# One level of Strassen's scheme for the first input projection of a two-layer decoder trunk

## The chip, the core and the metric

The kernel runs on one core of a Trainium2 chip. The time is device microseconds (us) for one execution of the whole program. TensorE (PE) multiplies, VectorE (DVE) and ScalarE (ACT) work elementwise and read the PSUM banks, GpSimd (POOL) works elementwise on SBUF, and SyncE (SP) issues transfers.

## The reference

The trunk has two layers over 512 tokens of width 1024, in float32. Layer 0 begins with the projection that the change rewrites: 1024 inputs to 7168 outputs, split into seven parts.

```python
def conv_gmlp_mixer(xn, w_in, conv_w, ln_g, ln_b, w_s, b_s, w_out):
    proj = xn @ w_in                       # 512 x 1024 times 1024 x 7168
    a_b, a_c, a_x, a_gate, b_u, b_v, b_gate = jnp.split(proj, EVEN_SPLITS, axis=-1)
    y_a = a_b * causal_short_conv(a_c * a_x, conv_w) * jax.nn.silu(a_gate)
    v = layernorm(b_v, ln_g, ln_b).reshape(bsz, n_chunks, B_CHUNK, B_GROUPS, B_GDIM)
    ...
    s = jnp.einsum('gts,bnsgc->bntgc', w_causal, v) + b_s[None, None, :, :, None]
    y_b = b_u * s.reshape(bsz, seq, B_WIDTH) * jax.nn.silu(b_gate)
    return jnp.concatenate([y_a, y_b], axis=-1) @ w_out
```

After it come an output projection, a gated per-layer embedding, and layer 1 (an mLSTM with its own projections), none of whose arithmetic changes.

## The kernel before

Every large product is done in three passes to keep float32 accuracy: a weight `w` is split into `w_hi` (its rounded form, `hi` on ACT, line 453) and `w_lo = w - w_hi` (`lo` on DVE, line 741), the activations likewise into `x_hi` and `x_lo`, and PE adds `hi*hi`, `hi*lo` and `lo*hi` in a PSUM bank.

Weights come in **slots** of 1 MB (128 partitions x 2048 numbers), 87 in all, two in flight (`raw`, `w_hi`, `w_lo` have two places). A slot is 48 matmuls of 128x128 weights against 512 columns. The first 28 slots are the projection: 4 token-major for `b_v` (the result has tokens on partitions, lines 1186 to 1188), then four groups of 4 feature-major slots (`a_c`, `a_x`, `a_gate`, `a_b`, lines 1172 to 1174, 256 features each), then four pairs (`b_gate`, `b_u`), between which PE does 8 small matmuls of the causal mix (line 1263). In feature-major form the convolution along the tokens needs no transpose. `tail(0)`, the output projection, follows.

Each engine's queue is written out by hand, and semaphores join them. `hi(s+2)` and `lo(s+2)` stand in the queues where the slot `s` is being finished, and wait for its last matmul. POOL does only tiny norm arithmetic (lines 384 to 386), the triangle mask of the mix weights (line 404), and so on. SP loads slot `s` when `lo(s-2)` is done.

At the start, the four token tiles of `x` are normalised (`h_square` on ACT, three POOL operations, `normalise` on DVE, line 764), transposed on PE (line 1201, 8 transposes a tile) and split (`x_high` line 473, `x_low` line 771); products of a tile start as soon as it is there.

## Time and profile before

| what | us |
|---|---|
| median of 3 runs | 1057.43 |
| lowest and highest of them | 1055.49 and 1058.51 |
| span of the profiled execution | 1055.9 |
| PE busy in it | 1033.2 (98%) |
| DVE busy | 505.8 (48%) |
| ACT busy | 325.0 (31%) |
| POOL busy | 57.3 (5%) |

The span is one execution under the profiler and lies inside the spread of the runs. A busy PE is not PE at its peak, since matmuls are pipelined and a row's duration (some 0.39 us) is longer than the distance from one matmul's start to the next; the starts are what counts.

### The profile page before, as it was taken

The page shows a single profiled execution, that of the slowest core. Times are in us where ns is not written, and L with a number is a line of the kernel's source. Part 1 is how long each engine was busy: PE and PEld are TensorE (multiplying, and loading weights), DVE is VectorE, ACT ScalarE, POOL GpSimd, SP SyncE. Part 2 cuts the span into 40 slices and gives each one's busy share as a digit, 9 for nine tenths or more (in the row PEclk, how much of TensorE's full clock was granted, in tenths as well). Part 3 has the DMA queues.
Part 4 walks back from the last instruction along what each step waited for, and adds up shares of the span by engine and source line. Part 5 has one row for each costly group of instructions (what it writes and reads, how often), then busy time and mean ns, then how long its engine had stood idle before and what let it go on. Part 6 is the DMA issues. An engine that isn't in the chain of part 4 may idle for free.

```text
span 1055.9 us, 12689 instructions
## 1 busy us (share of the span) xinstructions
PE 1033.2 (98%) x4702; PEld 854.6 (81%) x4702; DVE 505.8 (48%) x748; ACT 325.0 (31%) x556; POOL 57.3 (5%) x107
## 2 busy tenths in 40 slices
PE   6999999999999999998999999999999999999998
PEld 4888888888888888787888888888888888888876
DVE  5244454447664224656554453543355235441735
ACT  5221212122112124544332322332233222322622
POOL 2010000000000002203000000000000000000400
PEclk9999999999999999999999999999999999999999
DMA  7322232322322422221322222123222222143122
GB/s 299 120 92 108 80 120 79 116 82 80 104 95 70 180 109 80 80 95 65 120 80 81 80 80 108 55 81 112 82 79 79 79 80 80 40 180 120 41 80 79
DMA packets 17107, 102.22 MB, mean 97 GB/s; under 512 B 2096, under 2 KB 3120, under 8 KB 5936
## 3 DMA queue, kind: packets, MB, share of 16 engines
q1 hardware_dynamic: 17072, 101.74, 26.5%
q8 instruction: 24, 0.39, 0.2%
q14 instruction: 11, 0.09, 0.0%
HBM read 99.64 MB, written 2.10 MB: 96 GB/s over the span
## 4 chain that ended last, share of the span: by engine, by line
PE 93%; DVE 2%; POOL 2%; ACT 2%; issue 1%; DMA 1%; POOLq 0%; SPq 0%; DVEq 0%; ACTq 0%
PE bank L1174 17%; PE bank L1172 17%; PE bank L1173 17%; PE bank L1186 12%; PE bank L1188 12%; PE bank L1187 12%; PE bank L1415 1%; ACT square L464 1%; PE bank L1406 1%; PE bank L1418 1%; PE bank L1393 1%; POOL rstds L386 1%; PE bank L1263 1%; PE bank L1354 1%; POOL rstds L385 1%
## 5 line engine op out<-in xcount | busy, mean ns | idle before, releaser
L741 DVE TENSOR_TENSOR w_lo<-raw,w_hi 128x1024 fp32r<-128x1024 f32 x174 | 206.3, 1227 | 468.1 <-ACT w_hi L453 468.0
L453 ACT ACTIVATE w_hi<-raw 128x1024 fp32r<-128x1024 f32 x174 | 174.8, 1053 | 568.5 <-PE bank L1174 327.1
L1172 PE MATMUL bank<-x_hi,w_hi 128*128 128x512 f32 x776 | 305.2, 393 | 0.0
L1174 PE MATMUL bank<-x_hi,w_lo 128*128 128x512 f32 x776 | 302.3, 390 | 0.0
L1173 PE MATMUL bank<-x_lo,w_hi 128*128 128x512 f32 x776 | 302.2, 389 | 0.0
L1174 PEld LDWEIGHTS bank<-x_hi,w_lo 128*128 128x128 f32 x776 | 145.6, 188 | 30.5
L1173 PEld LDWEIGHTS bank<-x_lo,w_hi 128*128 128x128 f32 x776 | 145.7, 188 | 30.1
L1172 PEld LDWEIGHTS bank<-x_hi,w_hi 128*128 128x128 f32 x776 | 145.7, 188 | 29.7
L1186 PE MATMUL bank<-w_hi,x_hi 128*128 128x512 f32 x320 | 128.1, 400 | 0.6 <-DVE w_lo L741 0.5
L1187 PE MATMUL bank<-w_lo,x_hi 128*128 128x512 f32 x320 | 125.9, 393 | 0.0
L1188 PE MATMUL bank<-w_hi,x_lo 128*128 128x512 f32 x320 | 125.8, 393 | 0.0
L1186 PE MATMUL bank<-w_hi,y_hi 128*128 128x512 f32 x256 | 100.1, 391 | 0.0
L1188 PE MATMUL bank<-w_hi,y_lo 128*128 128x512 f32 x256 | 99.6, 389 | 0.0
L1187 PE MATMUL bank<-w_lo,y_hi 128*128 128x512 f32 x256 | 99.6, 389 | 0.0
L1186 PEld LDWEIGHTS bank<-w_hi,x_hi 128*128 128x128 f32 x320 | 61.0, 191 | 13.7 <-issue 0.8
L1188 PEld LDWEIGHTS bank<-w_hi,x_lo 128*128 128x128 f32 x320 | 60.9, 190 | 13.0
L1187 PEld LDWEIGHTS bank<-w_lo,x_hi 128*128 128x128 f32 x320 | 61.1, 191 | 12.4
L1188 PEld LDWEIGHTS bank<-w_hi,y_lo 128*128 128x128 f32 x256 | 48.0, 188 | 10.0
L1187 PEld LDWEIGHTS bank<-w_lo,y_hi 128*128 128x128 f32 x256 | 48.1, 188 | 9.9
L1186 PEld LDWEIGHTS bank<-w_hi,y_hi 128*128 128x128 f32 x256 | 48.1, 188 | 9.8
L384 POOL TENSOR_TENSOR rstds<-sums 128x1 f32<-128x1 f32 x24 | 12.0, 499 | 487.6 <-ACT square L464 487.6
L1201 PE MATMUL bank<-ident,scaled 128*128 128x128 f32 x128 | 19.0, 296 | 16.4 <-DVE scaled L764 12.7
(145 smaller groups left out, 755.5 us busy)
## 6 DMA issues: line engine op xcount, KB each, us to landing
...
```

The source lines that it names most:

```text
L384: link(pool.tensor_tensor(dst, first, second, ALU.add))
L385: link(pool.tensor_scalar(dst, dst, 1.0 / D, EPS, ALU.mult, ALU.add))
L386: pool.tensor_tensor(dst, dst, minus_half[:, 0:1], ALU.pow).then_inc(done, 1)
L453: act.activation(w_hi[:, r, c], raw[:, r, c], ACT.Copy).then_inc(hi_ready, 1)
L741: dve.tensor_tensor(w_lo[:, r, c], raw[:, r, c], w_hi[:, r, c].bitcast(F32), ALU.subtract).then_inc(lo_ready, 1)
L1172: pe.matmul(bank[b][:, :], w[0][:, k, at], x_hi[:, k], start=(k == 0), stop=False)
L1173: pe.matmul(bank[b][:, :], w[0][:, k, at], x_lo[:, k], start=False, stop=False)
L1174: done = pe.matmul(bank[b][:, :], w[1][:, k, at], x_hi[:, k], start=False, stop=(k == KD - 1))
L1186: pe.matmul(bank[b][:, :], hi_[:, k0 + k, tt], w[0][:, k, c], start=(start and k == 0), stop=False)
L1187: pe.matmul(bank[b][:, :], hi_[:, k0 + k, tt], w[1][:, k, c], start=False, stop=False)
L1188: done = pe.matmul(bank[b][:, :], lo_[:, k0 + k, tt], w[0][:, k, c], start=False, stop=(stop and k == ks - 1))
L1201: done = pe.transpose(bank[norm_bank(e, t) + q][:, k * P:(k + 1) * P], scaled[:, t % 2, (4 * q + k) * P:(4 * q + k + 1) * P], ident[:, :])
```

## The change

The projection becomes seven **units** of 1024 output columns. One unit is a 512 x 1024 times 1024 x 1024 product cut in half in each dimension, and computed with seven block products instead of eight. The weight quarters are called X, V, Z, Y (buffers `BX`, `BV`, `BZ`, `BY`). Products 1, 2 and 3 use X, Z and Y as loaded. The other four need block sums, made in place in `raw7`:

- product 5: X + V, by a POOL add of 128x2048 numbers
- product 6: that sum + Y, by a second POOL add
- product 7: V + Y, by a transfer from POOL's queue that adds Y onto V (`accum_op`)
- product 4: sum 6 + Z, by a second such transfer (`late_sum`)

A product is 24 matmuls of 512 columns (2 token tiles, 4 blocks of the inner dimension, 3 passes). It is token-major in all seven units, so x is the stationary side. The order in a unit is 1, 5, 6, 2, 3, 7, 4 (in the first 1, 2, 5, 6, 3, 7, 4). Weight splits (`hi7`, `lo7`) run two products ahead in a ring of three. The sums of results are kept in PSUM and in `s5`: `b_copy` and `s5_copy` on ACT, `c_make` and `s5_make` on DVE. `s5_make` reads product 7's result, and product 4 waits for it, which is next in PE's queue.

The seven left-side blocks (`l_hi`, `l_lo`) are made once at the start; four of them are sums and differences of x blocks made on DVE. Since `a_c * a_x` and the gates are now token-major, PE transposes them (`conv_transposes`, 8 for each of 8 feature tiles), and the mixed half as well (`mix_transposes`, 4 for each of 8). The causal mix is 8 matmuls of 512 columns instead of 32 of 128. The layer norm's scale and shift, on DVE before, are now 16 POOL operations of 128x512 (`ln_affine`). Two matmuls (`warm`) stand between the first two tiles' transposes. `h` is loaded again for the residual, because its place is used. The hi and lo of the mixer's outputs are made in the last unit and in `tail(0)`.

The weights of the projection are read as 4 MB for a unit as before, and the two adding transfers read 2 MB more. Nothing in layer 1 or in the output projection changes but where tensors lie.

The core of the diff:

```diff
+UNITS = 7
+ORDER_FIRST = (1, 2, 5, 6, 3, 7, 4)
+ORDER = (1, 5, 6, 2, 3, 7, 4)
+L_PLACE = {1: 0, 5: 1, 6: 2, 2: 3, 3: 4, 7: 5, 4: 6}
+RING = 3
+ROWS_IN = 4 * UNITS
+KIND = "vaaaabb"
...
+def source(u, p):
+    return {1: x_buffer(u), 5: s5_buffer(u), 6: x_buffer(u), 2: BZ, 3: BY, 7: BV, 4: x_buffer(u)}[p]
...
+        def block_in(u, b):
+            row_of = {BX: 0, BV: 1, BZ: 2, BY: 3}
+            sp.dma_start(raw7[:, x_buffer(u) if b == BX else b], slots[4 * u + row_of[b]]).then_inc(b_in[b], 16)
...
+        for u in range(UNITS):
+            sp.wait_ge(sum_done, sum_at(u, 6))
+            sp.wait_ge(w7_lo_ready, split_done(u, 5))
+            if u + 1 < UNITS:
+                block_in(u + 1, BX)
+            sp.wait_ge(w7_lo_ready, split_done(u, 2))
+            if u + 1 < UNITS:
+                block_in(u + 1, BZ)
+            sp.wait_ge(w7_lo_ready, split_done(u, 3))
+            if u + 1 < UNITS:
+                block_in(u + 1, BY)
+            else:
+                load(0, 0, wait=False)
+                load(1, 1, wait=False)
+            sp.wait_ge(w7_lo_ready, split_done(u, 7))
+            if u + 1 < UNITS:
+                block_in(u + 1, BV)
...
+        def add(u, p, dst, one, two):
+            if p == 5:
+                pool.wait_ge(b_in[BX], 16 * (u + 1))
+                pool.wait_ge(b_in[BV], 16 * (u + 1))
+                if u:
+                    pool.wait_ge(w7_lo_ready, split_done(u - 1, 4))
+            if p == 6:
+                pool.wait_ge(sum_done, sum_at(u, 5))
+                pool.wait_ge(b_in[BY], 16 * (u + 1))
+                pool.wait_ge(w7_lo_ready, split_done(u, 1))
+            pool.tensor_tensor(raw7[:, dst], raw7[:, one], raw7[:, two], ALU.add).then_inc(sum_done, 1)
+        def sums_of(u):
+            add(u, 5, s5_buffer(u), x_buffer(u), BV)
+            add(u, 6, x_buffer(u), s5_buffer(u), BY)
+            pool.wait_ge(sum_done, sum_at(u, 5))
+            pool.dma_start(raw7[:, BV], slots[4 * u + 3], accum_op=ALU.add).then_inc(added_in[7], 16)
+        def late_sum(u):
+            pool.wait_ge(w7_lo_ready, split_done(u, 6))
+            pool.dma_start(raw7[:, x_buffer(u)], slots[4 * u + 2], accum_op=ALU.add).then_inc(added_in[4], 16)
...
+                pool.wait_ge(ln_in, 32)
+                pool.wait_ge(vst_ready, TILES)
+            link(pool.tensor_tensor(v_even[:, g], v_even[:, g], over_tiles(ln_g), ALU.mult))
+            pool.tensor_tensor(v_even[:, g], v_even[:, g], over_tiles(ln_b), ALU.add).then_inc(ln_done, 1)
...
+            if p in SUMS:
+                act.wait_ge(sum_done, sum_at(u, p))
+            elif p in added_in:
+                act.wait_ge(added_in[p], 16 * (u + 1))
+            else:
+                act.wait_ge(b_in[BX if p == 1 else source(u, p)], 16 * (u + 1))
+            if g >= RING:
+                act.wait_ge(prod_done, 2 * (g - RING) + 2)
+            for half in range(2):
+                c = slice(half * SLOT // 2, (half + 1) * SLOT // 2)
+                act.activation(w7_hi[:, g % RING, c], raw7[:, source(u, p), c], ACT.Copy).then_inc(w7_hi_ready, 1)
...
+        def b_copy(u, tp):
+            act.wait_ge(prod_done, 2 * STEP[u, 1] + tp + 1)
+            if u:
+                act.wait_ge(b_free, 2 * (u - 1) + tp + 1)
+            else:
+                act.wait_ge(warm, 1)
+            act.activation(b_of(tp)[:, :], a_of(tp)[:, :], ACT.Copy).then_inc(b_copied, 1)
+        def s5_copy(u, tp):
+            act.wait_ge(prod_done, 2 * STEP[u, 5] + tp + 1)
+            if u:
+                act.wait_ge(s5_made if u == 1 else s5_free, s5_used(max(u - 1, 1), tp))
+            act.activation(s5[:, tp], c_of(tp)[:, :], ACT.Copy).then_inc(s5_copied, 1)
...
+        def lo7(g):
+            if g >= RING:
+                dve.wait_ge(prod_done, 2 * (g - RING) + 2)
+            for half in range(2):
+                c = slice(half * SLOT // 2, (half + 1) * SLOT // 2)
+                dve.wait_ge(w7_hi_ready, 2 * g + half + 1)
+                dve.tensor_tensor(w7_lo[:, g % RING, c], raw7[:, source(*STEPS[g]), c],
+                                  w7_hi[:, g % RING, c].bitcast(F32), ALU.subtract).then_inc(w7_lo_ready, 1)
...
+        def c_make(u, tp):
+            dve.wait_ge(s5_copied, 2 * u + tp + 1)
+            dve.wait_ge(prod_done, 2 * STEP[u, 6] + tp + 1)
+            dve.tensor_tensor(c_of(tp)[:, :], s5[:, tp], b_of(tp)[:, :], ALU.subtract).then_inc(c_made, 1)
+        def s5_make(u, tp):
+            dve.wait_ge(prod_done, 2 * STEP[u, 7] + tp + 1)
+            dve.wait_ge(c_made, 2 * u + tp + 1)
+            if KIND[u] == "v":
+                dve.tensor_tensor(v_even[:, 4:8, 2 + tp, :], s5[:, tp].rearrange("p (g c) -> p g c", g=4),
+                                  four(b_of(tp)), ALU.subtract).then_inc(s5_made, 1)
+            else:
+                dve.tensor_tensor(s5[:, tp], s5[:, tp], b_of(tp)[:, :], ALU.subtract).then_inc(s5_made, 1)
...
+            if k == 0:
+                left_sum(5, f5)
+                dve.wait_ge(full_ready[11], 2)
+                dve.wait_ge(full_ready[5], 2)
+                dve.tensor_tensor(f21[:, :, :], f11[:, :, :], f21[:, :, :], ALU.subtract).then_inc(full_ready[7], 1)
+                dve.wait_ge(full_ready[7], 1)
+                dve.tensor_tensor(f11[:, :, :], f5[:, :, :], f11[:, :, :], ALU.subtract).then_inc(full_ready[6], 1)
+                dve.wait_ge(full_ready[6], 1)
+                dve.wait_ge(full_ready[12], 2)
+                dve.tensor_tensor(f12[:, :, :], f11[:, :, :], f12[:, :, :], ALU.add).then_inc(full_ready[3], 1)
+                left_sum(6, f11)
...
+                if k == 3:
+                    for tp in range(2):
+                        c_make(u, tp)
+                if k == 6:
+                    s5_make(u, 1)
+                if g + 2 < 7 * UNITS:
+                    lo7(g + 2)
+                else:
+                    lo(k - 5)
...
+                if k == 4:
+                    for tp in range(2):
+                        if now == "a":
+                            z_make(u, a_of, tp, tp, a_free)
+                        else:
+                            wide_silu(u, a_of, tp, tp, a_free)
+                if was == "a" and k in (2, 4):
+                    conv(2 * (u - 2) + (k - 2) // 2)
...
+                if k == 5:
+                    s5_make(u, 0)
+                if k == 6:
+                    for tp in range(2):
+                        if now == "a":
+                            g_make(u, c_of(tp), tp, tp, c_free)
+                        else:
+                            gu_make(u, c_of(tp)[:, :], tp, tp, a_free, c_free)
...
+            first = p in (1, 5)
+            tt = slice(tp * P, (tp + 1) * P)
+            for k in range(4):
+                if tp == 0 and k % 2 == 0:
+                    pe.wait_ge(w7_lo_ready, 2 * g + k // 2 + 1)
+                c = slice(k * SEQ, (k + 1) * SEQ)
+                left_hi, left_lo = l_hi[:, L_PLACE[p], k, tt], l_lo[:, L_PLACE[p], k, tt]
+                pe.matmul(dst[:, :], left_hi, w7_hi[:, r, c], start=(first and k == 0), stop=False,
+                          skip_group_check=True)
+                pe.matmul(dst[:, :], left_hi, w7_lo[:, r, c], start=False, stop=False, skip_group_check=True)
+                done = pe.matmul(dst[:, :], left_lo, w7_hi[:, r, c], start=False, stop=(k == 3),
+                                 skip_group_check=True)
+            done.then_inc(prod_done, 1)
...
+            for t in range(TILES):
+                done = pe.transpose(bank[6][:, t * P:(t + 1) * P], z_tok[:, t, f * P:(f + 1) * P], ident[:, :])
+            done.then_inc(zt_ready, 1)
+            pe.wait_ge(c_free, 2 * v + 2)
+            pe.wait_ge(s5_free, s5_used(v, 1))
+            if n:
+                pe.wait_ge(y32_a, n)
+            for t in range(TILES):
+                done = pe.transpose(bank[7][:, t * P:(t + 1) * P], g_tok[:, t, f * P:(f + 1) * P], ident[:, :])
+            done.then_inc(gt_ready, 1)
...
+        first_transpose(0)
+        for tp in range(2):
+            done = pe.matmul(b_of(tp)[:, :], ident[:, :], h[:, 0, 0:SEQ], start=True, stop=True)
+        done.then_inc(warm, 1)
+        first_transpose(1)
+        product(0, 1, 0)
+        first_transpose(2)
+        product(0, 1, 1)
+        first_transpose(3)
+        for g in range(1, 7 * UNITS):
+            u, p = STEPS[g]
+            k = g % 7
+            if u and KIND[u - 1] == "a" and k in (2, 4):
+                conv_transposes(2 * (u - 2) + (k - 2) // 2)
+            if u == UNITS - 1:
+                if k >= 3:
+                    mix_transposes(k - 3)
+                if 2 <= k <= 5:
+                    mix(k - 2)
+            for tp in range(2):
+                product(u, p, tp)
...
+    def quarters(c1, c2):
+        for half in (slice(0, SEQ), slice(SEQ, D)):
+            for c in (c1, c2):
+                token(c, half, slice(0, SEQ))
```

**DVE, unit 3 of the projection (its feature group before).** Before, two slots of `lo`, and the convolution of two tiles:

```order
L741 TENSOR_TENSOR w_lo<-raw,w_hi 128x1024 [waits hi_ready,product_ready]
L741 TENSOR_TENSOR w_lo<-raw,w_hi 128x1024 [waits hi_ready]
L827 TENSOR_TENSOR conv_in<-bank,act_t 128x512 [waits act_freed,product_ready] x2
L836 TENSOR_SCALAR acc<-conv_in,conv_sb 128x512 [waits dve_freed]
L838 SCALAR_TENSOR_TENSOR acc<-conv_in,conv_sb,acc 128x512 [waits dve_step] x2
```

Now, from product 3 to product 4 of a unit (`s_85` is `s5`, `y_78` is `y32`; lines of the changed kernel):

```order
L1088 TENSOR_TENSOR w_lo<-raw_75,w_hi 128x1024 [waits w7_hi_ready,prod_done]
L1088 TENSOR_TENSOR w_lo<-raw_75,w_hi 128x1024 [waits w7_hi_ready]
L1165 TENSOR_TENSOR z_tok<-bank,ac_s 128x256 [waits zt_ready,ac_ready] x2
L1182 TENSOR_SCALAR y_78<-conv_in,conv_sb 128x512 [waits conv_ready]
L1184 SCALAR_TENSOR_TENSOR y_78<-conv_in,conv_sb,y_78 128x512 [waits dve_step] x2
L1186 TENSOR_TENSOR y_78<-y_78,bank 128x512 [waits gt_ready,dve_step]
L1088 TENSOR_TENSOR w_lo<-raw_75,w_hi 128x1024 [waits w7_hi_ready,prod_done]
L1088 TENSOR_TENSOR w_lo<-raw_75,w_hi 128x1024 [waits w7_hi_ready]
L1154 TENSOR_TENSOR s_85<-s_85,bank 128x512 [waits c_made,prod_done] x2
```

The step that PE waits for (line 1154) stands behind two splits and a convolution.

**POOL, after the first unit.** Before, behind the first tiles' norms stood one mask and more norm steps:

```order
L404 AFFINE_SELECT wt<-wt 128x1024 [waits const_in]
L408 TENSOR_SCALAR rstds<-bn_mv 128x1 [waits ln_stats]
L409 TENSOR_TENSOR rstds<-rstds,minus_half 128x1 [waits pool_step]
```

Now each unit has two wide adds and two transfers, and units 2, 3 and 4 have layer norm pairs too (`raw_75` is `raw7`):

```order
L521 TENSOR_TENSOR raw_75<-raw_75 128x2048 [waits w7_lo_ready,v_raw_in,x_raw_in]
L521 TENSOR_TENSOR raw_75<-raw_75 128x2048 [waits w7_lo_ready,y_raw_in,sum_done]
L527 DMA raw_75<-in_slots 128x2048 [waits sum_done]
L531 DMA raw_75<-in_slots 128x2048 [waits w7_lo_ready]
L558 TENSOR_TENSOR v_even<-v_even,ln_g 128x512 [waits vst_ready,ln_in]
L559 TENSOR_TENSOR v_even<-v_even,ln_b 128x512 [waits pool_step]
```

POOL's first add of unit u+1 waits for the weight split of product 4 of unit u, the first two rows of the DVE piece above.

**DVE at the start.** Before, between the fourth tile's scaling and the second slot's split:

```order
L764 SCALAR_TENSOR_TENSOR scaled<-h,rstds,g_pre 128x1024 [waits xt_ready,pre_rstd]
L771 TENSOR_TENSOR x_lo<-bank,x_hi 128x4x128 [waits xhi_ready] x2
L741 TENSOR_TENSOR w_lo<-raw,w_hi 128x1024 [waits hi_ready] x2
```

Now, up to the split of the third product's weights:

```order
L1095 SCALAR_TENSOR_TENSOR scaled<-h,rstds,g_first 128x1024 [waits first_xt,first_rstd]
L1108 TENSOR_TENSOR l_lo<-bank,l_hi 128x4x128 [waits lhs_hi4]
L1117 TENSOR_TENSOR f_83<-f_81,bank 128x4x128 [waits first_xt,full21_ready]
L1088 TENSOR_TENSOR w_lo<-raw_75,w_hi 128x1024 [waits w7_hi_ready] x2
L1108 TENSOR_TENSOR l_lo<-bank,l_hi 128x4x128 [waits lhs_hi4]
L1117 TENSOR_TENSOR f_83<-f_81,bank 128x4x128 [waits first_xt,full21_ready]
L1121 TENSOR_TENSOR l_lo<-f_83,l_hi 128x1024 [waits lhs_hi5]
L1220 TENSOR_TENSOR f_81<-f_80,f_81 128x1024 [waits full5_ready,full11_ready]
L1222 TENSOR_TENSOR f_80<-f_83,f_80 128x1024 [waits full7_ready]
L1225 TENSOR_TENSOR f_82<-f_80,f_82 128x1024 [waits full12_ready,full6_ready]
L1121 TENSOR_TENSOR l_lo<-f_80,l_hi 128x1024 [waits lhs_hi6]
L1121 TENSOR_TENSOR l_lo<-f_82,l_hi 128x1024 [waits lhs_hi3]
```

All of these come before the weights of the third product are split on DVE.

## Rows read from the trace of the kernel before

**Rows 1.** The page's parts 1 and 4: busy times, and the chain by engine.

```profile
PE 1033.2 (98%) x4702; PEld 854.6 (81%) x4702; DVE 505.8 (48%) x748; ACT 325.0 (31%) x556; POOL 57.3 (5%) x107
...
PE 93%; DVE 2%; POOL 2%; ACT 2%; issue 1%; DMA 1%; POOLq 0%; SPq 0%; DVEq 0%; ACTq 0%
```

**Rows 2.** Busy time by stretch: stretch, length, PE, PEld, DVE, ACT, POOL, clock, DMA.

```profile
142.00:183.00 41.00, 41.00 (x182) 33.95 (x182) 18.04 (x24) 8.08 (x10) 0.00 (x0) 1.00 0.29 102
```

**Rows 3.** Timeline, PE at the projection's end: start, duration, engine, line, operation.

```profile
330.61 0.39 PE L1186 MATMUL bank<-w_hi,y_hi 128*128 128x512 f32 x1
```

**Rows 4.** Timeline, ACT: weight splits, one for each finished slot.

```profile
192.80 2.01 ACT L453 ACTIVATE w_hi<-raw 128x1024 fp32r<-128x1024 f32 x2 [7.90 <-PE bank L1174]
203.68 2.01 ACT L453 ACTIVATE w_hi<-raw 128x1024 fp32r<-128x1024 f32 x2 [8.87 <-PE bank L1174]
...
294.57 2.00 ACT L453 ACTIVATE w_hi<-raw 128x1024 fp32r<-128x1024 f32 x2 [8.87 <-PE bank L1174]
...
318.13 2.00 ACT L453 ACTIVATE w_hi<-raw 128x1024 fp32r<-128x1024 f32 x2 [8.87 <-PE bank L1174]
```

**Rows 5.** Timeline, PE at the start.

```profile
17.95 0.63 PE L1188 MATMUL bank<-w_hi,x_lo 128*128 128x512 f32 x1
18.38 0.62 PE L1186 MATMUL bank<-w_hi,x_hi 128*128 128x512 f32 x1
...
19.07 0.39 PE L1188 MATMUL bank<-w_hi,x_lo 128*128 128x512 f32 x1
19.30 1.03 PE L1201 MATMUL bank<-ident,scaled 128*128 128x128 f32 x8
20.09 0.47 PE L1186 MATMUL bank<-w_hi,x_hi 128*128 128x512 f32 x1
20.40 0.39 PE L1187 MATMUL bank<-w_lo,x_hi 128*128 128x512 f32 x1
```

**Rows 6.** Groups by line and form: count, then busy us, mean ns, idle before.

```profile
L741 DVE TENSOR_TENSOR w_lo<-raw,w_hi 128x1024 fp32r<-128x1024 f32 x174 | 206.3, 1227 | 468.1 <-ACT w_hi L453 468.0
L453 ACT ACTIVATE w_hi<-raw 128x1024 fp32r<-128x1024 f32 x174 | 174.8, 1053 | 568.5 <-PE bank L1174 327.1 <-PE bank L1188 225.6 <-DMA raw<-in_slots 15.8
...
L771 DVE TENSOR_TENSOR x_lo<-bank,x_hi 128x512 fp32r<-128x512 f32 x32 | 20.4, 683 | 0.6 <-ACT x_hi L473 0.5
...
L464 ACT ACTIVATE square<-h 128x512 f32<-128x512 f32 x32 | 20.2, 630 | 10.4 <-DVE h L930 5.4 <-DMA h<-in_x 4.4
...
L473 ACT ACTIVATE x_hi<-bank 128x512 fp32r<-128x512 f32 x32 | 17.8, 613 | 9.0 <-PE bank L1201 9.0
...
L838 DVE SCALAR_TENSOR_TENSOR acc<-conv_in,conv_sb,acc 128x512 f32<-128x512 f32 x16 | 12.0, 752 | 1.9 <-DVE acc L836 0.5 <-DVE acc L838 0.2
...
L836 DVE TENSOR_SCALAR acc<-conv_in,conv_sb 128x512 f32<-128x512 f32 x8 | 3.9, 482 | 0.8 <-DVE acc L838 0.7
```

**Rows 7.** Timeline, DVE at the start.

```profile
16.39 1.28 DVE L764 SCALAR_TENSOR_TENSOR scaled<-h,rstds,g_pre 128x1024 f32<-128x1024 f32 x1 [1.00 <-POOL rstds L386]
17.59 1.28 DVE L771 TENSOR_TENSOR x_lo<-bank,x_hi 128x512 fp32r<-128x512 f32 x2
18.79 1.28 DVE L764 SCALAR_TENSOR_TENSOR scaled<-h,rstds,g_pre 128x1024 f32<-128x1024 f32 x1
...
22.00 3.28 DVE L741 TENSOR_TENSOR w_lo<-raw,w_hi 128x1024 fp32r<-128x1024 f32 x2
...
30.85 2.36 DVE L741 TENSOR_TENSOR w_lo<-raw,w_hi 128x1024 fp32r<-128x1024 f32 x2 [4.06 <-ACT w_hi L453]
```

**Rows 8.** Timeline, POOL at the start.

```profile
16.69 1.04 POOL L384 TENSOR_TENSOR rstds<-sums 128x1 f32<-128x1 f32 x1 [0.34 <-ACT square L464]
...
18.09 0.55 POOL L386 TENSOR_TENSOR rstds<-rstds,minus_half 128x1 f32<-128x1 f32 x1
...
21.97 1.10 POOL L404 TENSOR_SCALAR_AFFINE_SELECT wt<-wt 128x1024 f32<-128x1024 f32 x1 [3.34 <-DMA bias_sb<-in_gate_bias]
```

**Rows 9.** Transfers of the tile `raw`, window 95 to 330 us.

```profile
DMA to landing us min/median/max: 4.7/4.8/6.6
```

929 lines of the change are left out of this document (601 added, 328 removed).

## The prediction

> **What bounds the kernel now.** I read the busy times and the chain by engine first [rows 1]: PE is busy 98% of the span and the chain is PE for 93% of it. In the projection, PE is never idle in a 41 us stretch while DVE works 18.0 us and ACT 8.1 [rows 2]. So work taken from PE is worth its full time, as long as what PE waits for arrives. Next the pitch: one slot is finished every 203.68 - 192.80 = 10.88 us, that is 48 matmuls of 0.2267 us [rows 4]. The projection ends at 330.61, where the output projection's first matmul starts [rows 3]. Of that, 28 slots are 28 x 10.88 = 304.6. Two of the last slots with their 8 mix matmuls between take 318.13 - 294.57 = 23.56, so the mix costs 1.8 us, 7.2 in four groups [rows 4]. The remaining 330.6 - 304.6 - 7.2 = 18.8 us is the start: loads, norms, transposes, and matmuls that start 0.43 us apart (17.95 to 18.38) until 18.4 and 0.23 apart from about 19 [rows 5], the lower and the higher level of PE's clock.
>
> **PE's own work after the change.** 49 products of 24 matmuls are 49 x 5.44 = 266.6 us, 38.1 less. New are 96 transposes. Eight of them lie between the matmul start at 19.07 and the one at 20.09; less one matmul of 0.23, and with the next start 0.08 late, that is 0.87 us or 0.11 each [rows 5]: 10.5 us. The mix has the same number of columns, 7.2 us. Together 284.3 against 311.8, so **27.5 us less**, if nothing waits. The 16 transposes and 4 mix matmuls that now lie inside the output projection are in this sum. I cost the `y` splits there at nothing: four slots of products (43.5 us) lie over them, and ACT and DVE need under 15; without that cover it would be PE's wait for the last of them, some 3 us.
>
> **The start.** The third product (5) needs block sums of x, and in DVE's queue these stand before the split of its weights (last piece of the order). The third tile's scaling starts at 16.39 in the trace [rows 7]. Two more ACT copies (0.61 each [rows 6]) stand ahead of its squares; since POOL's steps there waited for DVE anyway, I add 0.4 of their 1.2. Behind its squares ACT now makes four copies before the fourth tile's two squares (0.63 each, 1.6 with their reads) [rows 6], so the fourth scaling starts at 16.8 + 2.4 + 1.6 = 20.8 (18.79 before [rows 7]). Then come in turn: the scaling 1.28, four PSUM-reading steps 2.73, a split 2.36, ACT's pass of 1.05, four DVE passes of 1.23 (4.9), ACT's next pass and half split 2.1, DVE's half split 1.2, gaps 0.5; 16.1 in all [rows 6, 7], while the two remaining `l_lo` passes run beside ACT. Product 5 starts at 37.0. Two products, 10.9 us, lie before it, so the start costs 26.1 instead of 18.8, **7.3 us more**. The two `warm` matmuls fall in the wait for the second tile; each is four times a mix matmul, 0.9 us, or 1.8 at the low clock, so their cost is up to 3.6 us, and their gain up to 2, if the first product then runs at the high one. I take zero.
>
> **The adds on POOL.** No row shows an add of 128x2048 on POOL. The nearest is the mask of 128x1024, with one input: 1.10 us [rows 8]. By it a 2048-wide operation is 2.1 us if both inputs come at once, and 4.2 if one after the other. I take 4.2, since the inputs are two; the lower bound is 2.1. GPSIMD Engine Reference, Instruction dispatch, in the Trainium skill says that both inputs share one read port and gives some 2.5 cycles per element; at its 1.2 GHz that is an estimate of 4.3 us for an add, and the sum below would be 0.7 higher by it. No run here shows it.
>
> What the adds do to DVE is in the trace. While the mask ran on POOL (21.97 to 23.07), two halves of `lo` took 3.28 us instead of 2.36 [rows 7, 8]: 0.92 lost of 1.10. The reverse too: POOL's tiny add at 16.69 took 1.04 us and ended with DVE's scaling (16.39 to 17.67), while the next, at 18.09, took its usual 0.55 beside DVE's `x_low` (17.59 to 18.87), which has a PSUM input [rows 7, 8]. So a DVE operation with two SBUF inputs, and a POOL operation, exclude each other; one with a PSUM input is free. By this, at the start, both adds (8.4 us), which start when the fourth tile's norm is done, fall into the DVE chain above; two PSUM-reading steps of 0.68 hide 1.4. **7.0 us more.**
>
> **Inside a unit.** With product 1 at 0, products end every 5.44, plus 0.9 for 8 transposes before the third and the fifth: product 3 ends at 29.0, product 7 at 34.4, where product 4 wants `s5_make`. DVE's queue there (the second piece of the order): the split for product 4 begins when ACT's `hi7` is half done behind its copies and the convolution's, at about 25.2, and ends at 27.6; two `z_make` of 0.43 (256 wide, from the 1024- and 512-wide rows) to 28.5; the convolution 0.48 + 2 x 0.75 + 0.68 and gaps, 3.1, to 31.6; the split 2.36 to 34.0; `s5_make` 0.68 to 34.7 [rows 6]. So without POOL PE waits some 0.2, over seven units 1.2.
>
> The next unit's first add waits for the split that ends at 27.6 and for V, whose load goes out after the split for product 7 (22.5) and lands 4.8 us later, at 27.3 [rows 9]. It holds DVE out from 27.7 to 31.9. `z_make` reads PSUM and goes on; the convolution starts at 31.9 instead of 28.5, **3.4 us late**, and so does `s5_make`, with no slack before it. Product 4 and what is behind it on PE wait 3.3. The second add falls after the last split and delays only work with over 5 us of slack. Five units (1 to 5) have a next unit and a convolution or a norm of like size there: 5 x 3.3 = **16.5**. In units 2 and 3, six POOL operations of the layer norm (1.1 each by the mask's row, for two inputs of a quarter of the add's width) alternate with DVE before `c_make`; I take 1.5 each, **3.0**, between 0 and 6.
>
> **Sum.** -27.5 + 7.3 + 7.0 + 16.5 + 3.0 + 1.2 = +7.5. The profiled span is 1055.9, so 1063.4; the median of the runs lies 1.5 above that span, so **1065**. Its own range is 1056 to 1075: the norm term, the 0.92 of 1.10, and the warm matmuls. That one 1.1 us operation keeps DVE out says little of a 4.2 us one: SBUF — State Buffer, Who interferes with whom, in the Trainium skill says that the port is held for the whole instruction. By that the forecast's sum holds; by a port that is handed over in between it would be the second rival's.
>
> **Rivals.**
> - *Short adds.* If an add takes 2.1, the start loses 2.8 instead of 7.0 and a unit 1.3 instead of 3.3; the norms 1. Then -27.5 + 7.3 + 2.8 + 6.5 + 1 + 1.2 = -8.7: 1049. For: half the width costs 1.1. Against: two inputs. V landing late (maximum 6.6 [rows 9]) does not help, since the add then meets the split; it must land 6 us late to miss `s5_make`.
> - *No exclusion in the place that counts,* since POOL's long operation lets DVE in, or DVE's slack is larger than I find. Only the start's chain stays: -27.5 + 7.3 + 1.2 = -19: 1038. Against it stand the 0.92 us.
> - *The adding transfers are late.* Their speed is in no row. A plain 1 MB lands in 4.8 us [rows 9]. The one for product 4 goes out after the split for product 6 (about 7) and `hi7` wants it at 23.9: 17 us of room, and it shares the engines with four plain loads a unit. From 17 us, 3.5 times a plain one, PE waits. At 20 us it is 3 us in each of six units, 18 on top of the forecast: 1083.
>
> **Chances.** Forecast 0.44, short adds 0.22, no exclusion 0.14, late transfers 0.20. A difference of 0.3% (3.2 us) is about what a measurement of this kernel can tell from no change. Faster by more (under 1054.3) holds all of the second rival and most of the first: 0.33. Within: 0.13, the rest of the first and the forecast's lower edge. Slower: 0.54. The range 1040 to 1084 leaves out about half of the second rival and some of the third.
>
> **What would show it.** The start: product 5's first matmul near 44 us if the adds hit, 37 if not. In a unit: POOL's row of the add near 4.2 us; DVE's `TENSOR_SCALAR` of the convolution starting when the add ends; PE idle 3 us before product 4, released by `s5_make`. PE waits of another kind, for `hi7` behind a transfer on POOL's queue, are the third rival. It would be wrong if the add is short, if PE's clock falls to its low level in the long waits at the start (24 matmuls there would cost 5 us more), or if the waits on PE come from ACT's copies, which I hid.

## The result, and the profile after

The changed kernel takes 1076.14 us (median of four runs, 1074.89 to 1076.47) against 1057.29 for the kernel before (median of four runs, one more than above): ratio 1.0183, 95% interval 1.0167 to 1.0198. It is 18.9 us slower, where 7.6 slower was forecast, and lies inside the wide range (1040 to 1084) but just above the forecast's own, 1056 to 1075. The profiled span is 1073.8 us, 17.9 above that of before, and the working below is made in spans.

The page's parts 1 and 4 of the changed kernel, beside [rows 1]:

```profile
PE 1021.1 (95%) x4586; PEld 836.7 (78%) x4586; DVE 618.4 (58%) x809; ACT 406.1 (38%) x680; POOL 162.3 (15%) x151
...
PE 84%; DVE 7%; issue 3%; ACT 3%; POOL 2%; DMA 0%; POOLq 0%; DVEq 0%; ACTq 0%
```

PE is busy 12 us less, yet the span is 18 longer: PE waits, and the chain now runs through DVE for 7% of the span. Two stretches say where, the one of [rows 2] and nearly the whole projection (stretch, length, PE, PEld, DVE, ACT, POOL, clock, DMA):

```profile
142.00:183.00 41.00, 37.77 (x168) 30.93 (x167) 34.22 (x34) 17.55 (x26) 20.33 (x10) 0.96 0.51 138
```

```profile
50.00:304.00 254.00, 233.49 (x1000) 190.56 (x999) 207.67 (x204) 106.65 (x146) 97.75 (x47) 0.94 0.51 140
```

PE has lost 3.2 of 41 us to waiting, DVE's busy time has gone from 18.0 to 34.2, and the granted clock is no longer 1.00. The waits of PE from 46 to 346 us (for what: us in total, times, longest):

```profile
PE bank L1697 <- DVE s L1154: 15.9, 5, 3.4
PE bank L1697 <- issue: 4.6, 2, 3.8
```

L1697 is a product's first kind of matmul, L1154 is `s5_make`: these are the five waits before product 4 that the prediction forecast. One of them in full, with what follows, on PE's timeline:

```profile
113.55 0.79 PE L1697 MATMUL bank<-w_hi,l_hi 128*128 128x512 f32 x1 [3.39 <-DVE s L1154]
114.14 0.63 PE L1699 MATMUL bank<-w_lo,l_hi 128*128 128x512 f32 x1
...
118.83 0.53 PE L1697 MATMUL bank<-w_hi,l_hi 128*128 128x512 f32 x1
119.20 0.40 PE L1699 MATMUL bank<-w_lo,l_hi 128*128 128x512 f32 x1
119.44 0.40 PE L1700 MATMUL bank<-w_hi,l_lo 128*128 128x512 f32 x1
```

From 114.14 to 118.83 the matmuls start 0.43 us apart, which is the level of 1.2 GHz; from 119.20 on 0.23 to 0.24 apart, that of 2.4 GHz. The 12 matmuls from 113.55 on take 118.83 - 113.55 = 5.3 us instead of 12 x 0.2267 = 2.7. So behind a wait of 3.39 us PE loses another 2.6 us. The prediction had no term for this.

What held `s5_make` in the next unit, on DVE's and on POOL's timeline:

```profile
148.98 0.75 DVE L1165 TENSOR_TENSOR z_tok<-bank,ac_s 128x256 f32<-128x256 f32 x2
149.65 0.48 DVE L1182 TENSOR_SCALAR y<-conv_in,conv_sb 128x512 f32<-128x512 f32 x1
150.16 5.78 DVE L1184 SCALAR_TENSOR_TENSOR y<-conv_in,conv_sb,y 128x512 f32<-128x512 f32 x2
155.97 0.69 DVE L1186 TENSOR_TENSOR y<-y,bank 128x512 f32<-128x512 f32 x1
156.58 2.35 DVE L1088 TENSOR_TENSOR w_lo<-raw,w_hi 128x1024 fp32r<-128x1024 f32 x2
158.85 1.28 DVE L1154 TENSOR_TENSOR s<-s,bank 128x512 f32<-128x512 f32 x2
160.05 5.84 DVE L1088 TENSOR_TENSOR w_lo<-raw,w_hi 128x1024 fp32r<-128x1024 f32 x2
```

```profile
149.96 4.64 POOL L521 TENSOR_TENSOR raw<-raw 128x2048 f32<-128x2048 f32 x1 [12.21 <-DMA raw<-in_slots]
159.10 4.57 POOL L521 TENSOR_TENSOR raw<-raw 128x2048 f32<-128x2048 f32 x1 [4.50 <-DVE w_lo L1088]
```

Two convolution steps that take 0.75 each alone [rows 6] take 5.78: the first of them waits for the end of the add at 154.60. The split at 160.05 waits in the same way for the second add. `s5_make`, which reads PSUM, starts at 158.85 and runs undisturbed past 159.10, the start of that add.

At the end of unit 0 the same, first POOL's row and then DVE's:

```profile
61.74 4.58 POOL L521 TENSOR_TENSOR raw<-raw 128x2048 f32<-128x2048 f32 x1 [12.67 <-DMA raw<-in_slots]
```

```profile
62.27 6.27 DVE L1088 TENSOR_TENSOR w_lo<-raw,w_hi 128x1024 fp32r<-128x1024 f32 x2
68.46 1.27 DVE L1151 TENSOR_TENSOR v_even<-s,bank 128x512 f32<-128x512 f32 x2
```

L1151 is unit 0's `s5_make`. PE waits 3.84 us for it before 69.24, listed under "issue" above.

The start, rows of PE, DVE and POOL that answer to [rows 5], [rows 7] and [rows 8]:

```profile
34.41 0.76 PE L1697 MATMUL bank<-w_hi,l_hi 128*128 128x512 f32 x1 [7.43 <-ACT bank L706]
...
42.37 0.47 PE L1697 MATMUL bank<-w_hi,l_hi 128*128 128x512 f32 x1 [0.93 <-DVE w_lo L1088]
```

```profile
19.37 5.58 DVE L1095 SCALAR_TENSOR_TENSOR scaled<-h,rstds,g_first 128x1024 f32<-128x1024 f32 x1 [0.57 <-POOL rstds L496]
...
26.07 5.47 DVE L1088 TENSOR_TENSOR w_lo<-raw,w_hi 128x1024 fp32r<-128x1024 f32 x2
```

```profile
19.30 10.02 POOL L521 TENSOR_TENSOR raw<-raw 128x2048 f32<-128x2048 f32 x2
```

A scaling of 1.28 us takes 5.58 and a split of 2.36 takes 5.47 while both adds run. Product 5 starts at 42.37. Last, the output projection's first matmul, which stood at 330.61 [rows 3]:

```profile
345.84 0.39 PE L1616 MATMUL bank<-w_hi,y_hi 128*128 128x512 f32 x1
```

So the projection is 15.2 us longer and all behind it, with its 16 transposes and 4 mix matmuls, 728.0 instead of 725.3.

### The profile page after: what moved, and what is told of

The parts are those of the page before. It is cut to its first block, busy times and chain, and to the rows that moved or that the text cites. A ratio compares the mean times of both kernels' runs of the same rounds, so it can differ in the third digit from the quotient of the medians.

```text
span 1073.8 us, 12432 instructions
## 1 busy us (share of the span) xinstructions
PE 1021.1 (95%) x4586; PEld 836.7 (78%) x4586; DVE 618.4 (58%) x809; ACT 406.1 (38%) x680; POOL 162.3 (15%) x151
## 4 chain that ended last, share of the span: by engine, by line
PE 84%; DVE 7%; issue 3%; ACT 3%; POOL 2%; DMA 0%; POOLq 0%; DVEq 0%; ACTq 0%
PE bank L1616 10%; PE bank L1618 10%; PE bank L1617 10%; PE bank L1599 8%; PE bank L1600 8%; PE bank L1601 8%; PE bank L1697 7%; PE bank L1700 7%; PE bank L1699 7%; DVE w_lo L1088 2%; ACT square L632 1%; PE bank L1927 1%; DVE y L1184 1%; PE bank L1918 1%; PE bank L1930 1%
## 5 line engine op out<-in xcount | busy, mean ns | idle before, releaser
L1047 DVE TENSOR_TENSOR w_lo<-raw,w_hi 128x1024 fp32r<-128x1024 f32 x118 | 139.2, 1221 | 314.9 <-ACT w_hi L621 314.9
L1697 PE MATMUL bank<-w_hi,l_hi 128*128 128x512 f32 x392 | 162.3, 414 | 28.9 <-DVE s L1154 15.9
L1088 DVE TENSOR_TENSOR w_lo<-raw,w_hi 128x1024 fp32r<-128x1024 f32 x98 | 152.0, 1592 | 50.5 <-ACT w_hi L659 49.9
L1700 PE MATMUL bank<-w_hi,l_lo 128*128 128x512 f32 x392 | 157.8, 403 | 0.0
L1699 PE MATMUL bank<-w_lo,l_hi 128*128 128x512 f32 x392 | 157.8, 402 | 0.0
L1599 PE MATMUL bank<-x_hi,w_hi 128*128 128x512 f32 x392 | 155.6, 397 | 0.0
L1601 PE MATMUL bank<-x_hi,w_lo 128*128 128x512 f32 x392 | 152.6, 389 | 0.0
L1600 PE MATMUL bank<-x_lo,w_hi 128*128 128x512 f32 x392 | 152.5, 389 | 0.0
L1697 PEld LDWEIGHTS bank<-w_hi,l_hi 128*128 128x128 f32 x392 | 77.2, 197 | 49.3 <-DVE s L1154 18.0
L1699 PEld LDWEIGHTS bank<-w_lo,l_hi 128*128 128x128 f32 x392 | 77.4, 197 | 16.8 <-issue 1.0
L1700 PEld LDWEIGHTS bank<-w_hi,l_lo 128*128 128x128 f32 x392 | 76.6, 195 | 16.8
```

Source lines behind the costliest of these rows:

```text
L1047: dve.tensor_tensor(w_lo[:, r, c], raw[:, r, c], w_hi[:, r, c].bitcast(F32), ALU.subtract).then_inc(lo_ready, 1)
L1088: dve.tensor_tensor(w7_lo[:, g % RING, c], raw7[:, source(*STEPS[g]), c], w7_hi[:, g % RING, c].bitcast(F32), ALU.subtract).then_inc(w7_lo ...
L1599: pe.matmul(bank[b][:, :], w[0][:, k, at], x_hi[:, k], start=(k == 0), stop=False)
L1600: pe.matmul(bank[b][:, :], w[0][:, k, at], x_lo[:, k], start=False, stop=False)
L1601: done = pe.matmul(bank[b][:, :], w[1][:, k, at], x_hi[:, k], start=False, stop=(k == KD - 1))
L1697: pe.matmul(dst[:, :], left_hi, w7_hi[:, r, c], start=(first and k == 0), stop=False, skip_group_check=True)
```

## Experiments

Each edit is made to the changed kernel (1076.14 us) unless another is named. Lines in the diffs are shortened to what counts; line numbers shift by a few from kernel to kernel.

### The adds of unit 0 alone, and those of the other units

```diff
+            w = 8 if u == 0 else SLOT      # the other kernel: u > 0
+            pool.tensor_tensor(raw7[:, dst, 0:w], raw7[:, one, 0:w], raw7[:, two, 0:w], ALU.add)
```

> In unit 0 both POOL adds are cut from 2048 to 8 columns (the weights of products 5 and 6 there are not the sums, so the output differs); all else as in the changed kernel (1076.1 us). Theory (in the start chain every POOL add keeps DVE out for its 4.6 to 5.4 us, and PE's clock falls to its low level in the waits that follow): product 5, whose first matmul was at 42.4 us, starts near 36, and the time is 6 to 8 us less, about 1069. Rival A (the start is bound by ACT's and DVE's own copies, the adds hidden beside them): product 5 still near 42, time within 1 us of 1076. Rival B (only the waits before product 4 matter): the same, 1076.

Measured: 1069.13 us, 7.0 less; product 5 starts at 35.14. The chain of the start, forecast at 37.0 without the adds and 44 with them, is shown in its parts: the adds cost 7.2 there.

> The twelve POOL adds of units 1 to 6 are cut to 8 columns (weights of products 5 and 6 there are not the sums); unit 0's stay. Theory: the five waits before product 4 (15.9 us together), the one at the end of unit 0 (3.8 at 69.2 us) and one of 0.7 at 54 go, less about 1.2 that DVE's queue costs by itself; with them goes what the low clock costs behind each (13 matmuls at 0.43 us for 0.23 is 2.7 us, three times that and three times about half of it, 12 in all): 31 us less, about 1045. Rival A (the waits cost only their own length, the low clock is made good elsewhere): 19 less, 1057. Rival B (DVE's queue is late by its own work, not by POOL): at most 4 less, 1072 or more.

Measured: 1044.12 us, 32.0 less, ratio to before 0.9876 (0.9858 to 0.9895). In this trace PE has no wait behind product 5 but two listed under "issue", 0.9 us together, and the granted clock of the same stretch is

```profile
50.00:304.00 254.00, 253.08 (x1146) 208.20 (x1145) 191.29 (x235) 128.16 (x176) 45.68 (x48) 1.00 0.59 160
```

Both rivals fall: DVE's queue is in time by itself, and the waits cost more than their length. Product 5 starts and the projection ends at

```profile
42.35 0.47 PE L1698 MATMUL bank<-w_hi,l_hi 128*128 128x512 f32 x1
...
312.25 0.39 PE L1617 MATMUL bank<-w_hi,y_hi 128*128 128x512 f32 x1
```

These 269.9 us are the 47 products with their transposes and mixes, and the 0.9 us of waits: 269.0 of work. Of those waits 0.77 us come before 54.24, and the changed kernel has the same one (0.74 before 54.27), so that one does not come from the adds of units 1 to 6. In the changed kernel the same stretch takes 345.84 - 42.37 = 303.5. That is 34.5 us over the work; 15.9 + 4.6 = 20.5 are waits, and 14.0 are left for the low clock.

### The waits filled

```diff
+                if 1 <= u < UNITS - 1 and tp == 0:
...
+                    for n in range(12):
+                        pe.matmul(bank[6][:, :], l_hi[:, L_PLACE[4], 0, 0:P], w7_hi[:, r, 0:SEQ], start=True, stop=True,
...
                 pe.wait_ge(s5_made, 2 * u + tp + 1)
```

> Nothing of the work is changed; in units 1 to 5 PE does 12 matmuls into an unused bank (12 x 0.227 = 2.7 us) before it waits for s5_make. Theory (PE's clock falls because PE stands idle in that wait): no low clock after the waits of units 1 to 5, matmuls behind product 4's start 0.23 us apart instead of 0.43, waits themselves shorter only by what the extra matmuls fill; 2.7 + 3 x 1.3 + 2.7 = 9 us less, about 1067. Rival A (the clock falls for another reason, such as the time since the start): the waits are filled but the granted clock still falls, 1076 or up to 3 more. Rival B (the extra matmuls run past the end of the wait): each adds up to 2 us, 1078 to 1086.

Measured: 1068.16 us, 8.0 less. PE at the place of the row of 113.55 above and at the projection's end, and the clock of the stretch:

```profile
109.92 2.88 PE L1693 MATMUL bank<-w_hi,l_hi 128*128 128x512 f32 x12
113.47 0.50 PE L1704 MATMUL bank<-w_hi,l_hi 128*128 128x512 f32 x1 [0.67 <-DVE s L1154]
113.81 0.40 PE L1706 MATMUL bank<-w_lo,l_hi 128*128 128x512 f32 x1
114.04 0.40 PE L1707 MATMUL bank<-w_hi,l_lo 128*128 128x512 f32 x1
...
336.09 0.39 PE L1616 MATMUL bank<-w_hi,y_hi 128*128 128x512 f32 x1
```

```profile
50.00:304.00 254.00, 246.12 (x1103) 201.76 (x1101) 217.39 (x212) 111.48 (x153) 100.79 (x48) 0.99 0.53 144
```

Sixty matmuls more, and the kernel is 8 us faster. Product 4 starts when it started before (113.47 for 113.55), but now at 0.23 us a matmul. The projection ends at 336.09 instead of 345.84, 9.8 us earlier; what lies behind it took 729.4 us in this trace instead of 727.9, with the same work, so the stretch says more here than the whole time.

The low clock can be counted on PE's timeline, as the distance from start to start, less idle time and less 0.2267 us, summed over the matmuls that start late behind a wait. In the changed kernel this gives 11.3 us behind the five waits (2.9, 1.9, 1.7, 1.6 and 3.2) and 2.9 behind that of unit 0. In e3 the five are down to 1.4, which is 9.9 less and as much as the projection gained; unit 0's wait was not filled, and 1.9 remain there. So the six waits account for all of the 14.0 us.

What a wait costs in this way is not fixed by its length. In the trace of e1 a wait of 3.39 us before 105.54, at the same place in unit 1 as the one before 113.55, is followed by matmuls 0.23 us apart and costs 0.3 us more, as in e3. What decides between 0.3 and 3.2 us is not shown by these runs.

### What stands in DVE's queue where the add falls

In the first kernel the first `s5_make` of a unit goes one place forward, ahead of the split for the next unit's product 1, and the convolution one place back, behind that split; the second `s5_make` stays where it was:

```diff
+                if k == 5:
+                    s5_make(u, 0)
                 if k == 6:
                     s5_make(u, 1)
                 if g + 2 < 7 * UNITS:
                     lo7(g + 2)
...
-                if was == "a" and k in (2, 4):
-                    conv(2 * (u - 2) + (k - 2) // 2)
+                if was == "a" and k in (2, 5):
+                    conv(2 * (u - 2) + k // 5)
```

> DVE's queue alone is changed: s5_make stands ahead of the split for the next unit's product 1, and the second convolution of a unit (in unit 1 the norm's last step) behind that split; the adds and everything else stay. Theory (the add's cost is one of place: it pushes what stands between it and s5_make): the six waits before product 4 or its like go, and with them the low clock, and the split for the next product 1 still ends over 2 us before it is wanted; 15.9 + 3.8 + 12 = 31 less, about 1045. Rival A (DVE as a whole has no room, the wait turns up before product 1 or 5 of the next unit as w_lo): half or less of it comes back, 1060 to 1076. Rival B (low clock not tied to these waits): 1057.

Measured: 1083.28 us, 7.1 more. A miss. PE's waits, and DVE and POOL in one unit:

```profile
PE bank L1697 <- DVE s L1154: 26.2, 5, 5.6
```

```profile
151.12 2.35 DVE L1088 TENSOR_TENSOR w_lo<-raw,w_hi 128x1024 fp32r<-128x1024 f32 x2
...
153.90 5.71 DVE L1184 SCALAR_TENSOR_TENSOR y<-conv_in,conv_sb,y 128x512 f32<-128x512 f32 x2
...
160.25 0.68 DVE L1154 TENSOR_TENSOR s<-s,bank 128x512 f32<-128x512 f32 x1
```

```profile
153.64 4.64 POOL L521 TENSOR_TENSOR raw<-raw 128x2048 f32<-128x2048 f32 x1 [2.42 <-DVE w_lo L1088]
```

Only the first `s5_make` had got ahead of the convolution. The second stood behind it, and the second add, released by the split that now stood ahead of the convolution, fell on the convolution. The next kernel moves both and leaves the convolution alone:

```diff
-                if k == 6:
+                if k == 5:
+                    s5_make(u, 0)
                     s5_make(u, 1)
                 if g + 2 < 7 * UNITS:
                     lo7(g + 2)
```

> Only DVE's queue is changed, and less of it than in e5: both s5_make stand ahead of the split for the next unit's product 1, the convolution stays where it was. e5 showed what happened there: its convolution stood ahead of the second s5_make, and the second add (153.64 to 158.28) fell on it. Theory: the first add still pushes the convolution, which then ends near 35.0 in a unit where product 4 wants s5_make at 34.4, so PE waits 0.7 to 1.5 us instead of 3.2, too short for the clock to fall; the second add falls behind both s5_make. 15.9 + 3.8 - 6 x 1.2 + 10 of low clock = 22 less, about 1054. Rival A (the second add now hits the splits of the next unit's products 1 and 5, which have no room): PE waits for w_lo there, 1065 or more. Rival B (the clock falls in waits of 1 us too): 1064.

Measured: 1062.31 us, 13.8 less where 22 were expected. The waits for `s5_make` are down to 3.0 us in two, but others have come: 6.2 us for the mix (`yb`) and 2.3 for the convolution (`y`). They are waits for DVE's late work, as in rival A, but not the ones for `w_lo` that it named, of which there are 0.5 us. Rival B's time is near, 1064, but not its reason: behind the two waits of 1.5 us for `s5_make` the matmuls start 0.23 us apart. In this place too, then, DVE's queue has no room for both adds. The next run tries a third place, behind both `s5_make`:

```diff
                     pool.wait_ge(w7_lo_ready, split_done(u - 1, 4))
+                    pool.wait_ge(s5_made, 2 * u)
```

> One wait more on POOL: the first add of units 1 to 6 waits for both s5_make of the unit before; DVE's queue is as in the changed kernel. Theory (the port is the matter, and where the adds fall sets the cost): no wait before product 4; both adds now lie at 35 to 44 us of a unit, in front of the splits for products 5 and 6 of the next, whose first halves are wanted at 45.3 and 50.7 and come at 45.3 and 50; PE waits 0 to 1.5 us a unit, 31 less plus 6 x 0.8: about 1050. Rival A (no room there either): over 2.5 us a unit and the clock falls again, 1068 or more. Rival B (the adds weren't what held s5_make): 1076.

Measured: 1069.35 us, 6.8 less, by the size that rival A named. Most of the waits have gone to bank c, whose last reader stands behind the split for product 5:

```profile
PE bank L1698 <- DVE g_tok L1173: 8.5, 4, 2.4
...
PE bank L1721 <- DVE y L1187: 4.1, 2, 2.1
```

### Is it the inputs that take POOL's time?

```diff
-            pool.tensor_tensor(raw7[:, dst], raw7[:, one], raw7[:, two], ALU.add)
+            pool.tensor_scalar(raw7[:, dst], raw7[:, one], 1.0, None, ALU.mult)
```

> Each of the 14 POOL adds becomes a multiplication by 1.0 of the same 128x2048, with one input instead of two (the sums are left out, so the output differs). If POOL's time goes by the inputs that it reads, one takes 2.2 to 2.4 us instead of 4.6 (the mask's 128x1024 took 1.10), the waits before product 4 fall from 3.2 to about 1 us, the clock stays high, and the start loses 4.5: about 27 less, 1049. If it goes by the elements written, it takes 4.6 and the time stays at 1076.

Measured: 1077.92 us (two runs). Neither forecast of the operation's length holds: it is longer than the add, with a median of 5.37 us (4.58 for the add):

```profile
L521 POOL TENSOR_SCALAR raw<-raw 128x2048 f32<-128x2048 f32 x14 | 77.1, 5508 | 108.9 <-DVE w_lo L1088 71.0 <-DMA raw<-in_slots 37.7
```

Whether two inputs cost twice as much can't be read from this form, but my reason for 4.2 us, twice the mask's rate because there are two inputs, has lost its ground: another operation with one input takes more. That the figure came out near the add's was luck as far as this reason goes.

### Smaller pieces

```diff
+            for q in range(4):
+                c = slice(q * SEQ, (q + 1) * SEQ)
+                done = pool.tensor_tensor(raw7[:, dst, c], raw7[:, one, c], raw7[:, two, c], ALU.add)
```

> Each add of the changed kernel is four of 128x512 in a row, the first start and the last end as one. If the two engines take turns and neither's work overlaps the other's, DVE's five operations with SBUF inputs between the split and s5_make meet all four pieces one after the other: the same 4.6 us, the same waits, 1076 within 2 us, with DVE's convolution steps each some 1.1 us longer instead of one 4 us longer. If shorter pieces let DVE run beside them, the waits before product 4 fall below 2 us and the clock stays high: 1060 or less.

Measured: 1063.84 us (two runs, 1063.18 and 1064.51), 12.3 less, between the two forecasts. DVE, then POOL (six pieces in one row), in the unit that follows 178 us:

```profile
185.87 2.46 DVE L1187 SCALAR_TENSOR_TENSOR y<-conv_in,conv_sb,y 128x512 f32<-128x512 f32 x2
188.36 0.69 DVE L1189 TENSOR_TENSOR y<-y,bank 128x512 f32<-128x512 f32 x1
188.96 3.83 DVE L1091 TENSOR_TENSOR w_lo<-raw,w_hi 128x1024 fp32r<-128x1024 f32 x2
```

```profile
186.14 11.39 POOL L523 TENSOR_TENSOR raw<-raw 128x512 f32<-128x512 f32 x6 [12.67 <-DMA raw<-in_slots]
```

The convolution pair loses 2.46 - 1.54 = 0.9 us and the split 3.83 - 2.36 = 1.5, 2.4 together where a whole add took 4.2 from the convolution pair alone. This is the mildest unit of the trace for PE: one unit earlier the same steps lose 1.9 and 1.5, 3.3 together. The two engines take turns, and the pieces that fall under DVE's steps with a PSUM input (0.69 us here, and `s5_make`) cost it nothing. With a whole add those steps stand in the queue behind the blocked one and hide nothing. The waits for `s5_make` fall from 15.9 to 11.1 us, and the one at the end of unit 0 from 3.84 to 0.40; the low clock behind them falls too.

### The adds by DVE itself

DVE makes the first sum of the next unit behind the second `s5_make`, the second behind the two steps that free bank c:

```diff
+                if k == 6 and u + 1 < UNITS:
+                    add(u + 1, 5)
+                    for tp in range(2):
+                        g_make(u, c_of(tp), tp, tp, c_free)    # or gu_make
+                    add(u + 1, 6)
                 lo7(g + 2)
```

> The same sums, all made by DVE: the first of the next unit behind the second s5_make, the second behind the two steps that free bank c; POOL keeps its transfers and norms. Theory (POOL's add holds DVE out for 4.6 us, while DVE would need two halves' 2 x 1.2 = 2.4 us for it): 2.2 us less of DVE's time for each add, and none of it ahead of s5_make; no wait before product 4, PE waits under 0.5 us a unit; at the start the chain before product 5 carries one add of 2.4 instead of 10 us: product 5 near 37.5. 32 less for the units and 5 for the start, about 1040. Rival A (DVE has no room, its queue is what binds): waits for w_lo or bank b before products 1, 5 or 6, 1060 or more. Rival B (POOL runs beside DVE at no cost and takes work from it): 1076 + 14 x 2.4 x the share on the path, over 1080.

Measured: 1040.82 us, ratio to before 0.9841 (0.9815 to 0.9866). It beats both kernels, and 1040 was forecast. At the start, where DVE makes unit 0's two adds among its passes, product 5 starts at 35.91 instead of 42.37. Of PE's waits from 46 to 350 us one is left, before product 3 of unit 0 and not before a product 4:

```profile
PE bank L1706 <- issue: 2.8, 1, 2.8
```

And DVE's adds in one unit:

```profile
138.65 1.38 DVE L1154 TENSOR_TENSOR s<-s,bank 128x512 f32<-128x512 f32 x2
139.94 2.28 DVE L1089 TENSOR_TENSOR raw<-raw 128x2048 f32<-128x2048 f32 x1
...
143.72 2.28 DVE L1089 TENSOR_TENSOR raw<-raw 128x2048 f32<-128x2048 f32 x1
```

An add costs DVE 2.28 us when DVE makes it. When POOL makes it, DVE's operations in the rows above take 3.1 to 4.3 us longer. Giving the adds to POOL spared DVE nothing.

### The start

In the first kernel, on top of e8, ACT's two `b_copy` go ahead of the pass for product 5, and the splits for products 5 and 6 come right behind what these need. The second adds to it that `s5_copy` and `c_make` of unit 0 no longer stand behind the split for product 7.

```diff
-                left_sum(5, f5)
                 b_copy(0, 0)
                 b_copy(0, 1)
+                left_sum(5, f5)
+                hi7(2)
                 left_sum(6, f11)
+                hi7(3)
```

> e8 with the start in another order. ACT makes the two bank copies ahead of the pass for product 5's left side, in e8 they stood behind it and PE waited 4.4 us for them (26.96). On DVE and ACT the splits of product 5's and 6's weights come right behind what those products need, the later sums of x behind them. Theory (the start is bound by the queues of DVE and ACT, step by step): product 2 starts near 24.2, after a wait of under 2 us and at the high clock; product 5 near 30 instead of 35.9; product 6 waits for its split until 38, 3.3 less than in e8: 1037.5. Rival A (something else, such as the copies themselves, binds): as e8, 1041. Rival B (product 3 then waits for what was put back, as long as was gained): 1040 to 1044.

Measured: 1041.31 us, as e8. Product 5 starts at 30.14, as forecast (35.91 in e8), but rival B is what happened, in PE's row at product 3:

```profile
50.41 0.77 PE L1712 MATMUL bank<-w_hi,l_hi 128*128 128x512 f32 x1 [6.40 <-DVE bank L1147]
```

In e8 product 3 starts at 50.16. All that was gained before it was lost in one wait for `c_make`.

```diff
                 left_sum(3, f12)          # DVE
+                c_make(0, 0)
+                c_make(0, 1)
```

> e9, and in unit 0 ACT copies product 5's bank right behind the split of product 3's weights, and DVE makes both c_make ahead of the split for product 7's; in e9 the first c_make stood behind it, at 49.62, and PE waited 6.4 us for it from 43.9. Theory (the start's gain of e9 was given back in that one wait): product 3 starts near 45 instead of 50.3, and no wait over 2.5 us follows; 5 less, 1036. Rival A (the next step of the chain, the split of product 7's weights or its left side, is as late): 1039 to 1041. Rival B (what PE gains here it loses before product 4 of unit 0, where V's transfer sets the pace): 1041.

Measured: 1035.00 us, ratio to before 0.9803 (0.9789 to 0.9817), the fastest. Product 3 starts at 45.42, and of PE's waits behind 20 us these are left, and 0.2 under "issue":

```profile
PE bank L1711 <- DVE w_lo L1076: 3.0, 2, 2.5
PE bank L1711 <- ACT bank L691: 1.3, 1, 1.3
```

Last, on the changed kernel itself, the warm matmuls in another place:

```diff
-        done = pe.matmul(b_of(tp)[:, :], ident[:, :], h[:, 0, 0:SEQ], start=True, stop=True)
         first_transpose(1)
         product(0, 1, 0)
         first_transpose(2)
         product(0, 1, 1)
+        done = pe.matmul(b_of(tp)[:, :], ident[:, :], h[:, 0, 0:SEQ], start=True, stop=True)
         first_transpose(3)
```

> The changed kernel with its two warm matmuls moved from ahead of the second tile's transposes to ahead of the fourth's, where PE waits 3.5 us. They must run somewhere, since product 6 adds onto a bank that ACT has filled. Theory (the prediction's zero: what they win by raising the clock early, PE later stands waiting for): the first product's matmuls start 0.43 apart, it ends 2.5 us later, and all of it is lost in the wait for the fourth tile; product 5 at 42.4 as before and 1076 within 1 us. Rival (an early high clock is worth its time): 1078 to 1079.

Measured: 1075.37 us, the same within the spread (1074.65 to 1079.90). The first product's matmuls start 0.43 apart from 15.09 to 17.22 (0.23 in the changed kernel), and PE still waits for the fourth tile (0.83 us before 25.05, where it was 3.50 before 25.00). Product 5 starts at 42.42, where it was 42.37. The zero for the warm matmuls was right. The profiled execution is the longest of the four, but what makes it longer lies behind the start: 731.2 us behind the projection instead of 727.9, with the same work, and 0.6 more in the wait at the end of unit 0.

## Why the prediction was right or wrong

The direction, and the mechanism and place of the waits, were right, and the time lies in the range (1040 to 1084). The size was not: 18.9 us instead of 7.6. The terms of the sum, each against what the traces give:

| term | forecast | measured | from |
|---|---|---|---|
| PE's own work | -27.5 | -29.2 | 269.0 in e2 + 2 x 5.44 + 2.7 behind the projection - 311.8 |
| start, with both adds | +14.3 | +12.7 | (42.37 - 10.9) - 18.8 |
| five waits before product 4 | +16.5 | +15.9 | the row of waits |
| end of unit 0 | none for the add | +3.8 | the wait before 69.24 |
| DVE's queue without adds | +1.2 | +0.7 | the wait before 54.27, in e2 too |
| norm pairs ahead of `c_make` | +3.0 | 0 | no wait for `c_make` |
| low clock behind the waits | none | +14.0 | 303.5 - 269.0 - 20.5 |
| sum | +7.5 | +17.9 | the spans differ by 17.9 |

**The step that failed** is the sum's treatment of a wait as its own length. The prediction did have the low clock, but only in what would prove it wrong, for the start, at 5 us; the five waits of 3.3 us that it forecast were never tested against it. Behind each of them, and behind that of unit 0, PE ran at 1.2 GHz for a while, 14.0 us in all. e3 shows the link: with PE kept at work in five of them, the clock stays up, the projection ends 9.8 us earlier and the kernel is 8.0 faster. This one term is larger than the whole miss of 10.4 us between the sum and the spans.

**The second miss** is unit 0. It also has a next unit, whose first add falls on a split ahead of its `s5_make`. I counted units 1 to 5 and left unit 0 at the 0.2 us of a unit without a convolution: 3.8 us more, in part made up for by the norm term of 3.0, which cost nothing. The operations of the norm are there and longer than forecast (1.85 to 1.91 us in the mean, 1.1 forecast), but PE never waits for a `c_make` of units 2 and 3.

**What held.** The exclusion of a POOL operation and a DVE one with two SBUF inputs, read off a single row of 1.10 us [rows 7, 8], holds for 4.6 us: 5.78 for two steps of 0.75. SBUF — State Buffer, Who interferes with whom, in the Trainium skill speaks of a hold for a whole instruction; the rows of the whole add agree, and e11 shows turns at the borders of instructions. The add's 4.2 us (measured 4.55 to 4.64 in the units, 5.38 at most at the start) was right in size. GPSIMD Engine Reference, Instruction dispatch, in the Trainium skill has some 2.5 cycles per element for two inputs on one read port; the estimate of 4.3 us made from it agrees with the median of 4.58 within 7%. My own derivation, two times a mask with one input, has no support left after e6. The start's chain was right to 1.6 us, and its part without adds to 1.9 (product 5 at 35.14 for 37.0). Of these, 1.2 come from the fourth scaling, which starts at 19.56 in e1 instead of 20.8.

Two of the prediction's signs of being wrong did show at the start, without a price there. PE waited 7.43 us for ACT's copy, and the next six matmuls ran at the low level; but product 5 then still waited 0.93 us for the split of its weights, so DVE's chain set its start, as forecast.

**The rivals.** Short adds: no, 4.58 us. No exclusion: no, DVE's operations with two SBUF inputs wait beside both adds, and without them (e2) the waits before product 4 are gone. Late transfers: the adding ones land in 8.2 us in the median, within the 17 that they had, and no wait of PE leads back to one:

```profile
raw<-in_slots SPq DMA_DIRECT2D x87, 1024.0 KB, 4.8
raw<-in_slots POOLq DMA_DIRECT2D x14, 1024.0 KB, 8.2
```

What stays open: what decides how long PE runs at the low level behind a wait of a given length; and why e4 and e7 lose more in the later units than I had worked out.
